# mLSTM layer of a hybrid decoder step: old-state products in runs of 16, head work ahead of the unit's split, an out-projection that begins before its last head

## What is computed

```python
num = w_inter * (q @ C_old) + (weights * (q @ k.T)) @ v
den = w_inter * (q @ n_old) + sum(weights * (q @ k.T))
h   = num / max(abs(den), exp(-m))
C_new = decay * C_old + (w_k * k).T @ v
out = (head_rms(h) * g_head * sigmoid(o)) @ w_out
```

## Time and profile before

| | |
|---|---|
| median of 3 runs | 2870.57 us (2869.45 to 2872.04) |
| the profiled execution's own time | 2872.99 us |
| its span, first to last instruction | 2871.0 us |
| TensorE busy | 2738.6 us, 95% |
| VectorE, ScalarE, GpSimd busy | 1302.4, 893.4, 193.6 us |
| granted TensorE clock, mean | 0.965 |
| `ML_O`, from the first to the last matmul of its units | about 538 to 646 us |
| `ML_OUT` | 674.5 to 745.8 us |
| K and V stages, layers 0 and 1 | about 796 to 871 and 2284 to 2360 us |

### The profile page before, as it was taken

One profiled execution on the slowest core, in us unless ns is written; L12 is line 12 of the kernel. 1 busy time (PEld: TensorE's weight loads), 2 busy tenths in 40 slices (PEclk: granted clock), 3 DMA queues, 4 the chain that ended last, 5 costly groups with the idle time before them and its releaser, 6 DMA issues.

```text
span 2871.0 us, 49901 instructions
## 1 busy us (share of the span) xinstructions
PE 2738.6 (95%) x21498; PEld 2625.3 (91%) x21498; DVE 1302.4 (45%) x2082; ACT 893.4 (31%) x1125; POOL 193.6 (7%) x169
## 2 busy tenths in 40 slices
PE   7999999998979999999999999998998889999999
PEld 7999999877876999999999999998987876999998
DVE  5444234234574444432444424777334573444422
ACT  4332222233323333322222222543323232333322
POOL 2000000011110100000000000001311000100000
PEclk9999999997999999999999999999978989999999
DMA  4333334122483233332333332223213472333331
GB/s 120 93 90 104 93 90 104 45 60 67 132 275 121 73 89 93 92 101 80 88 91 92 103 89 70 74 63 88 45 52 103 145 238 96 89 90 93 99 100 51
DMA packets 472628, 278.58 MB, mean 97 GB/s; under 512 B 24821, under 2 KB 460790, under 8 KB 472459
## 3 DMA queue, kind: packets, MB, share of 16 engines
q1 hardware_dynamic: 449720, 230.83, 28.4%
q0 software_dynamic: 8704, 33.56, 3.3%
q10 hardware_dynamic: 14078, 12.35, 1.4%
HBM read 259.21 MB, written 17.69 MB: 96 GB/s over the span
## 4 chain that ended last, share of the span: by engine, by line
PE 86%; DVE 5%; ACT 3%; issue 3%; DMA 1%; POOL 0%; ACTq 0%; SPq 0%; DVEq 0%; POOLq 0%
PE ACC L429 24%; PE ACC L431 24%; PE ACC L430 24%; PE ACC L1115 2%; PE M L2119 1%; ACT w_hi L512 1%; PE ACC L2119 1%; DVE w_lo L518 1%; PE M L1449 1%; PE M L1474 1%; DVE cache L1211 1%; PE M L2258 1%; PE M L2196 1%; DMA raw<-in_xa_w_k 1%; PE M L1519 1%
## 5 line engine op out<-in xcount | busy, mean ns | idle before, releaser
L429 PE MATMUL ACC<-xg_hi,w_hi 128*128 128x260 f32 x3968 | 1132.6, 285 | 11.6 <-DVE w_lo L890 7.6
L431 PE MATMUL ACC<-xg_hi,w_lo 128*128 128x260 f32 x3968 | 1126.6, 284 | 0.0
L430 PE MATMUL ACC<-xg_lo,w_hi 128*128 128x260 f32 x3968 | 1123.2, 283 | 0.0
L518 DVE TENSOR_TENSOR w_lo<-raw,w_hi 128x1024 fp32r<-128x1024 f32 (+1 forms) x326 | 421.9, 1294 | 1060.4 <-ACT w_hi L512 1054.5
L429 PEld LDWEIGHTS ACC<-xg_hi,w_hi 128*128 128x128 f32 x3968 | 753.3, 190 | 13.4 <-issue 8.6
L430 PEld LDWEIGHTS ACC<-xg_lo,w_hi 128*128 128x128 f32 x3968 | 752.6, 190 | 0.0
L431 PEld LDWEIGHTS ACC<-xg_hi,w_lo 128*128 128x128 f32 x3968 | 752.3, 190 | 0.0
L512 ACT ACTIVATE w_hi<-raw 128x1024 fp32r<-128x1024 f32 (+1 forms) x326 | 363.6, 1115 | 1234.4 <-PE ACC L431 1223.6
L430 PE MATMUL ACC<-hid_lo,w_hi 128*128 128x260 f32 x1408 | 398.3, 283 | 0.0
L431 PE MATMUL ACC<-hid_hi,w_lo 128*128 128x260 f32 x1408 | 397.6, 282 | 0.0
L429 PE MATMUL ACC<-hid_hi,w_hi 128*128 128x260 f32 x1408 | 397.4, 282 | 0.0
(11 more groups left out here) (549 smaller groups left out, 3307.7 us busy)
## 6 DMA issues: line engine op xcount, KB each, us to landing
raw<-in_ffn_w_gate SPq DMA_DIRECT2D x88, 512.0 KB, 3.8
raw<-in_ffn_w_up SPq DMA_DIRECT2D x88, 512.0 KB, 3.8
raw<-in_ffn_w_down SPq DMA_DIRECT2D x64, 704.0 KB, 4.5
cache<-in_cache_mem_k POOLq DMA_DIRECT2D x16, 1024.0 KB, 7.2
cache<-in_cache_mem_v POOLq DMA_DIRECT2D x16, 1024.0 KB, 6.7
raw<-in_gd_w_in SPq DMA_DIRECT2D x32, 512.0 KB, 4.1
raw<-in_ml_w_in SPq DMA_DIRECT2D x24, 512.0 KB, 3.9
raw<-in_xa_w_q SPq DMA_DIRECT2D x16, 512.0 KB, 4.5
```

Source lines behind the costliest of these rows:

```text
L429: pe.matmul(out, wh, hi[:, k0 + k, m], start=begin, stop=False)
L430: pe.matmul(out, wh, lo[:, k0 + k, m], start=False, stop=False)
L431: mm = pe.matmul(out, wl, hi[:, k0 + k, m], start=False, stop=end)
L518: dve.tensor_tensor(w_lo[:, j % 2, 0:n], raw[:, (j + d) % 4, 0:n], w_hi[:, j % 2, 0:n].bitcast(F32), ALU.subtract).then_inc(w_split, 1)
```

## The change

Products with old states: `state_query` computes one half of a head (16 matmuls). Head 1's halves stand at `ML_V`'s units 4 and 5, those of heads 2, 0 and 3 in `ML_O`: one ahead of each of the first three value products, the other at chunk 2 of units 2, 4 and 6, through a new hook `low`. Head 3's state is placed in the columns of V that heads 0 and 1 have left, and both loads move one step or more forward. Square sums of heads 0 to 2: GpSimd adds the two halves first.

Order: a new hook `first` on ScalarE and VectorE runs ahead of a unit's split; the heads' squares, copies and probabilities go there. The samples' outputs and sums move into `ML_O`. Head 2's gated product moves from GpSimd to VectorE. `ML_OUT` waits for heads 0 to 2 and the samples, and for head 3 at chunk 5 of its unit 0. The outer products and updates 0 to 3 move one unit later, 4 and 5 both stand in unit 5.

Attention, both layers: `spread(b)` moves to chunk 5 of unit 4 + b, the scores behind that unit, and what follows them one or two units later; the cached values are grouped 1, 2, 1, 2, 2.

```diff
 ml_Cst = gm_raw[:].rearrange("p c t -> p (c t)").rearrange("p (h e) -> p h e", h=MLH)
 ml_C0 = nc.alloc_sbuf_tensor_at("ml_C0", [P, NS, 256], F32, offset=rest + 16384)
 ml_C2 = nc.alloc_sbuf_tensor_at("ml_C2", [P, NS, 256], F32, offset=at_c2)
-ml_C3 = nc.alloc_sbuf_tensor_at("ml_C3", [P, NS, 256], F32, offset=rest)
...
+            if k == 2 and j in low:
+                low[j]()
...
     def step(i, j, last):
+        if first and 4 * i + j in first:
+            first[4 * i + j]()
         split_ahead(act_split, act, ph, i, j, last)
         if ph.kind == "gateup" and j % 2 == 0:
...
-VAL = [[0, 1], [2], [3, 4], [5, 6], [7]]
-at_pe = steps("at_pe", ["memT", "q8"] + [("qb", b) for b in range(7)] + [("kvN", 0), ("qb", 7), ("kvN", 1), "sT", "pT8"]
+VAL = [[0], [1, 2], [3], [4, 5], [6, 7]]
+at_pe = steps("at_pe", ["memT", "q8"] + [("qb", b) for b in range(6)] + [("kvN", 0), ("qb", 6), ("kvN", 1), ("qb", 7), "sT", "pT8"]
...
-    k = {3 + b: lambda b=b: spread(b) for b in range(5)}
-    v = {0: lambda: spread(5), 1: lambda: spread(6), 2: lambda: spread(7)}
-    k_mid = {1: by_token}
-    v_mid = {1: lambda: pe_kv_natural(pe, l, 0), 2: lambda: pe_kv_natural(pe, l, 1), 3: sample_turned, 6: sample_probs}
-    return k, k_mid, v, v_mid
+    k = {4 + b: lambda b=b: spread(b) for b in range(4)}
+    k[1] = by_token
+    v = {0: lambda: spread(4), 1: lambda: (spread(5), pe_kv_natural(pe, l, 0)),
+         2: lambda: (spread(6), pe_kv_natural(pe, l, 1)), 3: lambda: spread(7), 5: sample_turned, 7: sample_probs}
+    return k, v
...
     def bound():
-        dve_k_low(dve, l)
         at_pe.wait(dve, "sT", r=l)
...
-    k.update({3 + b: lambda b=b: sample_scores(b) for b in range(5)})
-    v = {b: lambda b=b: sample_scores(5 + b) for b in range(3)}
-    v.update({3: bound, 5: probs, 6: spaced})
+    k.update({4 + b: lambda b=b: sample_scores(b) for b in range(4)})
+    v = {b: lambda b=b: sample_scores(4 + b) for b in range(4)}
+    v.update({4: lambda: dve_k_low(dve, l), 5: bound, 6: probs, 7: spaced})
...
     def C_of(self, h):
-        return [ml_C0[:], tails[:, :, KC * P:KC * P + 256], ml_C2[:], ml_C3[:]][h]
+        return [ml_C0[:], tails[:, :, KC * P:KC * P + 256], ml_C2[:]][h]
+
+    def C_one(self, h, b):
+        return ml_vN[:, b // 2, (b % 2) * 256:(b % 2 + 1) * 256] if h == 3 else self.C_of(h)[:, b, :]
+
+    def C_parts(self, ext, h):
+        if h < 3:
+            return [(self.C_of(h), ext.rearrange("b p e -> p b e"))]
+        v = ext.rearrange("(t a) p e -> a p t e", a=2)
+        return [(ml_vN[:, :, a2 * 256:(a2 + 1) * 256], v[a2]) for a2 in range(2)]
...
     def c_load(self, eng, h):
-        eng.dma_start(self.C_of(h), a["state_mlstm_C"][0, :, h].rearrange("b p e -> p b e")).then_inc(ml_cin[h], 16)
+        for place, ext in self.C_parts(a["state_mlstm_C"][0, :, h], h):
+            eng.dma_start(place, ext).then_inc(ml_cin[h], 16)
 
...
         def outputs(h):
-            ml_dve.wait(pe, "PT", h)
             if h == 0:
                 ml_act.wait(pe, "vN", 7)
             else:
                 ml_dve.wait(pe, "ms", h - 1)
+            if h < MLH - 1:
+                self.state_query(pe, [2, 0, 3][h], 0)
+            ml_dve.wait(pe, "PT", h)
...
         v[4] = lambda: (value_rows(3), ml_dve.wait(pe, "kw", 3), self.state_query(pe, 1, 0))
-        v[5] = lambda: (value_rows(4), self.state_query(pe, 2, 16), sample_norm())
+        v[5] = lambda: (value_rows(4), self.state_query(pe, 1, 1), sample_norm())
+        def sample_sums():
+            ml_dve.wait(pe, "sq8")
+            ml_pe.done(pe.matmul(M[:, 3, 64:128], ones[:], ml_t8[:, 8, :], start=True, stop=True), "nsq8")
         q = {0: lambda: (value_rows(7), scores(0)), 1: lambda: (outputs(0), state(2, 4, 2))}
         for h in range(1, MLH):
             q[2 * h] = lambda h=h: (self.squares(pe, h - 1), scores(h))
-            q[2 * h + 1] = lambda h=h: (outputs(h), self.spread(pe, h - 1))
+            q[2 * h + 1] = lambda h=h: (outputs(h), self.spread(pe, h - 1), sample_sums() if h == MLH - 1 else None)
+        low = {2 * n + 2: lambda h=h: self.state_query(pe, h, 1) for n, h in enumerate((2, 0, 3))}
+        return {2: lambda: ml_pe.done(pe_gates(pe, 0), "gates"), 7: small_rows}, v, q, low
+
+    def state_query(self, pe, h, e):
+        pe.wait_ge(ml_cin[h], 16 * (1 + h // 3))
+        at = 16 * [2, 0, 1, 3][h] + e * NS
+        for b in range(NS):
+            mm = pe.matmul(M[:, 3, at + b:at + b + 1], self.C_one(h, b)[:, e * P:(e + 1) * P],
+                           pm[:, h, LP + b:LP + b + 1], start=True, stop=True)
+        ml_pe.done(mm, "hs", h, e)
...
     def squares(self, pe, h):
-        ml_act.wait(pe, "sq", h)
+        halved = h < MLH - 1
+        if halved:
+            ml_pool.wait(pe, "sa", h)
+        else:
+            ml_act.wait(pe, "sq", h)
         for b in range(TB):
-            for e in range(2):
-                mm = pe.matmul(M[:, 3, 4 + b:5 + b], self.sq()[:, e * TB + b], ones[:, 0:1], start=e == 0, stop=e == 1)
+            for e in range(1 if halved else 2):
+                mm = pe.matmul(M[:, 3, 4 + b:5 + b], self.sq()[:, e * TB + b], ones[:, 0:1],
+                               start=e == 0, stop=halved or e == 1)
         ml_pe.done(mm, "nsq", h)
...
     def pe(self, pe):
-        self.state_query(pe, 0, 16)
         self.squares(pe, MLH - 1)
         ml_dve.wait(pe, "cp", MLH - 1)
         for c in range(KC):
@@ -1498,11 +1526,8 @@
         ml_pe.done(mm, "v8")
         ml_dve.wait(pe, "n", MLH - 2)
         self.spread(pe, MLH - 1)
-        self.state_query(pe, 3, 32)
-        ml_dve.wait(pe, "sq8")
-        ml_pe.done(pe.matmul(M[:, 3, 64:128], ones[:], ml_t8[:, 8, :], start=True, stop=True), "nsq8")
         ml_pool.wait(pe, "yl", MLH - 2)
-        ml_dve.wait(pe, "yl", MLH - 1)
+        ml_dve.wait(pe, "y8")
...
-        return {n: lambda n=n: outer(n) for n in range(8)}
+        u = {n + 1: lambda n=n: outer(n) for n in range(4)}
+        u[0] = lambda: ml_dve.wait(pe, "yl", MLH - 1)
+        u[5] = lambda: (outer(4), outer(5))
+        u[6] = lambda: outer(6)
+        u[7] = lambda: outer(7)
+        return u
...
         def load_last():
-            ml_pe.wait(act, "num", MLH - 1)
+            ml_pe.wait(act, "num", 1)
             self.c_load(act, 3)
...
-        q = {0: lambda: values(7), 1: lambda: (squares(0), states(1), weights(1)),
-             2: lambda: (store_states(), load_first(), self.gate(act, 0)), 3: lambda: (squares(1), weights(2)),
-             4: lambda: self.gate(act, 1), 5: lambda: (squares(2), weights(3)),
-             6: lambda: (self.gate(act, 2), self.high(act, 0)), 7: lambda: (load_last(), squares(3), self.high(act, 1))}
-        return qk, v, q
+        first = {2 * h + 1: lambda h=h: squares(h) for h in range(MLH)}
+        q = {0: lambda: values(7), 1: lambda: (states(1), load_first(), weights(1)),
+             2: lambda: (store_states(), self.gate(act, 0)), 3: lambda: (load_last(), weights(2)),
+             4: lambda: (self.gate(act, 1), self.high(act, 0)), 5: lambda: weights(3),
+             6: lambda: (self.gate(act, 2), self.high(act, 1))}
+        return qk, v, q, first
...
     def high(self, act, h):
-        if h < MLH - 1:
+        if h < MLH - 2:
             ml_pool.wait(act, "y", h)
         else:
             ml_dve.wait(act, "y", h)
-        if h == 1 or h == 3:
-            ml_pe.wait(act, "S", MLH - 1)
+        ml_pe.wait(act, "S", MLH - 1 if h > 0 else 1)
         ml_act.done(act.activation(ml_y_hi[:, 2 * h:2 * h + 2, 0:LP], pm[:, 16 + 2 * h:18 + 2 * h, 0:LP], ACT.Copy), "yh", h)
 
     def act(self, act, own):
         self.gate(act, MLH - 1)
-        self.high(act, 2)
         ml_pe.wait(act, "v8")
         ml_act.done(act.activation(ml_v8t[:].rearrange("p (a b) -> p a b", a=2), M[0:NS, 0:2, :], ACT.Copy), "v8")
         ml_dve.wait(act, "ms8")
         ml_act.done(act.activation(ml_t8[:, 11, 0:32], ml_t8[:, 10, 0:32], ACT.Sqrt), "r8")
+        self.high(act, MLH - 2)
...
-        return {0: lambda: self.diagonal(act, 1), 2: lambda: (self.diagonal(act, 2), self.c_store(act, ML_UPD[0])),
-                4: lambda: (self.diagonal(act, 3), self.c_store(act, ML_UPD[1])), 6: lambda: self.c_store(act, ML_UPD[2]),
-                7: lambda: self.c_store(act, ML_UPD[3])}
+        return {0: lambda: self.diagonal(act, 1), 2: lambda: self.diagonal(act, 2), 3: lambda: self.c_store(act, ML_UPD[0]),
+                4: lambda: self.diagonal(act, 3), 5: lambda: self.c_store(act, ML_UPD[1]),
+                6: lambda: self.c_store(act, ML_UPD[2]), 7: lambda: self.c_store(act, ML_UPD[3])}
...
-        q = {0: lambda: (probs(0), masked(1)), 1: lambda: copied(0),
-             2: lambda: (self.means(dve, own, 0), probs(1), masked(2)), 3: lambda: (copied(1), self.normed(dve, 0)),
-             4: lambda: (self.means(dve, own, 1), probs(2), masked(3)), 5: lambda: (copied(2), self.normed(dve, 1)),
```

(69 more changed lines are left out.)

50 lines of the change are left out of this document (20 added, 30 removed), and 21 rows, old and new, of tables (ml_act, ml_dve, ml_pe).

## The result

The changed kernel takes 2843.68 us (median of 4 runs, 2840.46 to 2844.08) against 2871.11 us for the kernel before (4 runs); the ratio is 0.9903, 95% interval 0.989 to 0.9916. Its profiled span is 2841.6 us against 2871.0, the mean granted clock 0.969 against 0.965, TensorE busy 2729.2 us against 2738.6. The forecast was 2840, the range 2828 to 2858. The executions of a kernel differ by the places at which TensorE's clock falls to half, so a stretch read from one profile can differ in another by some us.

A forecast was written before the change was run, and what follows sets the result against it. TensorE, busy nearly all the time, was taken as the bound, with waits, narrow products and half clock to save. Terms -8 + 0 - 15.4 + 5.0 - 13 = -31.4 gave 2841.6 profiled, 2839.2 as median, stated as 2840; range 2828 to 2858.

The forecast's parts named there:

- Old-state products in the V stage: V stage: two full runs become two halves, -4.8, and fewer clock falls, -3.4; -8 us in all.
- Gate stage: Gate projection: added halves against shorter square sums, removed waits and two clock falls left; 0 us, between -3 and +9.
- Handover: Last gate unit to first out-projection matmul: a chain through four engines of 13 us instead of 28.45, -15.4.
- I let the gated product wait for the root: Handover: VectorE's gated product waits for GpSimd's root (1.0 us) by the port lock; with the rule 13 us, without 11.5.
- Out-projection: Units 5 and 6: new waits of 0.7 and 2.6 us for state updates, plus clock; +5.0 us, bounds +3 and +8.
- one fall of the clock (1.7) behind it: Out-projection: one fall of TensorE's clock to half behind the new waits, costing 1.7 us.
- Attention: K and V stages, both layers: later spread amid a unit evens the score groups' pace; -13 us, bounds -4 and -20.
- the first group's delay: Attention: the first score group comes a unit later, costing +1 to +4 us.
- The floor of 59 us: Attention: transfers at share 1.00, 317 GB/s, move the same bytes in 59 us, a least stage length.
- Rival B: K and V stages: transfers hold them, so attention gives only -4; sum -22, 2848 us; chance 0.15.
- Rival A: V, gate and out-projection stages: the clock falls nearly each time at narrow runs; -16, 2854 us; chance 0.17.
- rival C: Gate stage: the clock goes to half at the first halves and doesn't return; slower, 2893 us; chance 0.03.

The follow-up runs named there:

- no_first: The changed kernel with ScalarE's squares and VectorE's copies and probabilities behind split and eviction again, probabilities still ahead of the head's mean; 2851.15 us (0.9917).
- upd_first: The changed kernel with VectorE's state updates ahead of the unit's split instead of behind its eviction; median 2837.9 us (0.9846).
- attn_only: The kernel before with only the attention part of the change (spread, scores, grouping of the values); median 2862.96 us (0.9934).

## Why the prediction was right, step by step

The time was right to 4 us, and the kernel is faster, as forecast. Of the steps some were right; attention was out of its bounds, the out-projection was mis-sized, and a loss in unchanged code was not foreseen. That these cancel to 2 us in the sum is luck.

- *Old-state products in the V stage* (-8): right, -6.8 and -9.9 in two profiles of the kernel. The count of matmuls is sure, the falls are not. I had the first fall gone and half of the second left; in the first profile both are there, but half as long as before (3.4 us at half clock instead of 6.8), in the second neither is.
- *Gate stage* (0, two falls left, 0.5 for each of three heads): right, +0.6, with two falls and 0.6 for three heads. The number of falls was in part luck: the ten profiles with this gate stage have one to three. That the probabilities ahead of the split take the waits away is right in size (`no_first`, +7.8); left out was that the wait without it would be the mean's.
- *Handover* (13 us): 11.15. The step that failed is "I let the gated product wait for the root". It started at 643.88, the root at 644.04, and it was the root that took 1.93 us instead of 1.0. It stands beside the chain. So the chain lost 1.1 of the 1.85 us; the rest is small terms, the norm ready 0.3 earlier and the small operations and hand-overs shorter than taken. The stall for the samples did come, as forecast: their cast took 2.22 us beside GpSimd's subtraction, and their low part ended 0.3 us behind it. The price that the forecast gave for a chain without stalls at the port was 11.5.
- *Out-projection* (+5.0): the waits are exact (0.7 and 2.7 for 0.7 and 2.6). Mis-sized is the term "one fall of the clock (1.7) behind it": there are two, and each costs 3.1 (unit 5: 5.74 less 1.98 for the moved product and 0.70 of waiting; unit 6: 5.81 less 2.71), since the outer product itself then takes 3.78 us instead of 1.98 and the dense matmuls behind it are at half clock for some 2.7 us more. 6.2 for 1.7; the runs show that unit 6's comes with the idle (`upd_first`) and that unit 5's comes without it too, while two outer products stand in a row.
- *Attention* (-13, bounds -4 and -20): -21.6, out of its bounds. The mechanism was right, the pace that I took between 4.2 and 5.0 us was 4.2, and no fall of the clock is left. Mis-sized were the pace, at its good end, and the first group's delay, taken as +1 to +4 and measured as +0.5 and +0.6; what follows the last group gave -6.5 and -5.3 for the -5 taken. The floor of 59 us was wrong as well: it scaled the old stage's mean rate of 276 GB/s by its share to 317, and the engines moved 325 and had less to move inside the stage (56.2 us x 325 GB/s is 18.3 MB, 67.9 x 276 was 18.7). Rival B had the transfers hold the stages at -4. They hold only the first units (ScalarE's waits of 7.4 and 6.7 us), and the gain is -21.6.
- *Code that is not changed* (0, not thought of): +7.7. No step of the prediction allowed for it: it took code that is not edited as worth nothing, without a reason. Rival A came nearest, with falls of the clock inside the changed stages only. The loss comes with the attention part (`attn_only`, +7.9); why is open. It is what brought the sum back into place: -8.6 of attention and -2.2 of the handover and -1.1 in the setup against +7.7 here, +4.6 in the out-projection and +1.8 in V and gate stages.

The slower case (rival C) has nothing for it: no stretch at half clock in the changed kernel's gate stage lasted over 8 us.
